# Routing's choice in two parts, norms of window units ahead of maxima, and weight splits behind the second block's norms

## The reference, cut to what matters

```python
D_MODEL, SEQ, DEPTH = 1024, 512, 2
M_GROUPS, M_PER_GROUP, M_TOPK, M_HIDDEN = 4, 8, 2, 512      # 32 experts

def first_block(x, ...):
    alpha, h = (2 * DEPTH) ** 0.25, x
    for i in range(DEPTH):
        y = swa_sink_gqa(h, ...) if i == 0 else mla(h, ...)   # window attention; latent attention
        h = layer_norm(alpha * h + y, ln_g[i, 0], ln_b[i, 0])
        y = hier_moe(h, ...)
        h = layer_norm(alpha * h + y, ln_g[i, 1], ln_b[i, 1])
    return h

def hier_moe(x, w_group, w_expert, w_gate, w_up, w_down):
    p_group = jax.nn.softmax((xt @ w_group).astype(jnp.float32), axis=-1)
    g_w, g_idx = lax.top_k(p_group, 1)
    e_logits = (xt @ w_expert).astype(jnp.float32).reshape(n_tok, M_GROUPS, M_PER_GROUP)
    e_logits = e_logits[jnp.arange(n_tok), g_idx[:, 0]]
    e_w, e_idx = lax.top_k(jax.nn.softmax(e_logits, axis=-1), M_TOPK)
    weight = g_w * e_w / jnp.sum(e_w, -1, keepdims=True)
    expert = (g_idx * M_PER_GROUP + e_idx).reshape(-1)
    ...  # tokens sorted by expert, silu(x w_gate) * (x w_up) @ w_down per expert, summed per token

def second_block(x, ...):
    for l in range(DEPTH):
        h = rms_norm_2(x, norm_mix_pre[l])
        ...  # h @ w_in, four mixers side by side, mix = concatenation @ w_out
        x = x + rms_norm_2(mix, norm_mix_post[l])
        f = conv_ffn(rms_norm_2(x, norm_ffn_pre[l]), ffn_up[l], ffn_conv_w[l], ffn_down[l])
        x = x + rms_norm_2(f, norm_ffn_post[l])
    return x

def reference(...):
    return second_block(first_block(x, ...), ...)
```

## Time and profile before

| | |
|---|---|
| median of 3 runs | 2722.62 us (2719.04, 2725.57, 2722.62) |
| the profiled execution | 2721.77 us |
| its span, first to last instruction | 2719.9 us |
| mean granted clock of TensorE | 0.976 |
| PE busy | 2500.8 us, 92% |
| PE weight loads busy | 1849.2 us, 68% |
| DVE busy | 1074.3 us, 39% |
| ACT busy | 753.2 us, 28% |
| POOL busy | 181.6 us, 7% |
| DMA traffic | 576.56 MB, mean 212 GB/s |

### The profile page before, as it was taken

One profiled execution on the slowest core, in us unless ns is written; L12 is line 12 of the kernel. 1 busy time (PEld: TensorE's weight loads), 2 busy tenths in 40 slices (PEclk: granted clock), 3 DMA queues, 4 the chain that ended last, 5 costly groups with the idle time before them and its releaser, 6 DMA issues. The chain is left out here.

```text
span 2719.9 us, 36818 instructions
## 1 busy us (share of the span) xinstructions
PE 2500.8 (92%) x14582; PEld 1849.2 (68%) x14582; DVE 1074.3 (39%) x1596; ACT 753.2 (28%) x1217; POOL 181.6 (7%) x302
## 2 busy tenths in 40 slices
PE   8997998887898979998877999999999999999998
PEld 7675665544476666654444777888887877888887
DVE  4753100100345641110001666655543566555542
ACT  3530000000245410000001353443432444433421
POOL 0001111111000001111111010000000010000000
PEclk9998999999999989999999999999999999999999
DMA  6239999999722189999998412223233212223231
GB/s 170 83 136 379 405 404 407 411 408 407 264 93 78 40 332 406 402 406 408 407 411 338 159 62 83 82 94 99 93 124 108 84 49 96 84 94 99 93 124 54
DMA packets 174825, 576.56 MB, mean 212 GB/s; under 512 B 20496, under 2 KB 104016, under 8 KB 125042
## 3 DMA queue, kind: packets, MB, share of 16 engines
q1 hardware_dynamic: 164146, 558.07, 54.1%
q0 software_dynamic: 10560, 16.81, 1.9%
HBM read 569.56 MB, written 23.07 MB: 218 GB/s over the span
## 5 line engine op out<-in xcount | busy, mean ns | idle before, releaser
L1310 PE MATMUL ps<-first_weights,moe_xsT 128*64 128x256 f32 x2688 | 311.7, 381 | 50.0 <-DMA first_weights<-in_moe_w_up 30.7
L232 PE MATMUL ps<-l_h_hi,l_w_hi 128*128 128x512 f32 x896 | 353.4, 394 | 0.0
L234 PE MATMUL ps<-l_h_hi,l_w_lo 128*128 128x512 f32 x896 | 349.2, 390 | 0.0
L233 PE MATMUL ps<-l_h_lo,l_w_hi 128*128 128x512 f32 x896 | 349.1, 390 | 0.0
L1389 DVE TENSOR_TENSOR moe_hid<-moe_silu,ps 128x256 f32<-128x256 f32 x64 | 27.0, 421 | 781.4 <-PE ps L1310 781.4
L1310 PEld LDWEIGHTS ps<-first_weights,moe_xsT 128*64 128x64 f32 x2688 | 224.1, 137 | 147.5 <-issue 97.8
L2837 DVE TENSOR_TENSOR l_w_lo<-l_raw,l_w_hi 128x2048 fp32r<-128x2048 f32 x76 | 174.1, 2293 | 270.1 <-ACT l_w_hi L2598 270.1
L1362 ACT ACTIVATE moe_ys<-ps 128x512 f32<-128x512 f32 x64 | 38.2, 597 | 684.3 <-PE ps L1328 684.3
L1328 PE MATMUL ps<-first_weights,moe_hidT 128*64 128x512 f32 x672 | 172.1, 658 | 38.7 <-DVE moe_hidT L1391 38.7
L2598 ACT ACTIVATE l_w_hi<-l_raw 128x2048 fp32r<-128x2048 f32 x76 | 145.5, 1918 | 179.5 <-PE ps L234 168.4
L232 PEld LDWEIGHTS ps<-l_h_hi,l_w_hi 128*128 128x128 f32 x896 | 168.3, 188 | 37.3 <-issue 2.9
(11 more groups left out here) (578 smaller groups left out, 4344.2 us busy)
## 6 DMA issues: line engine op xcount, KB each, us to landing
first_weights<-in_moe_w_up SPq DMA_DIRECT2D x84, 1024.0 KB, 28.6
first_weights<-in_moe_w_down SPq DMA_DIRECT2D x84, 1024.0 KB, 28.7
first_weights<-in_moe_w_gate SPq DMA_DIRECT2D x84, 1024.0 KB, 27.9
first_ring<-in_moe_w_up SPq DMA_DIRECT2D x44, 1024.0 KB, 28.7
first_ring<-in_moe_w_down SPq DMA_DIRECT2D x44, 1024.0 KB, 28.5
l_raw<-in_ffn_up SPq DMA_DIRECT2D x44, 1024.0 KB, 5.1
first_ring<-in_moe_w_gate SPq DMA_DIRECT2D x40, 1024.0 KB, 28.2
l_raw<-in_w_in SPq DMA_DIRECT2D x22, 1024.0 KB, 5.2
```

The lines of the kernel that those rows point to most:

```text
L232: pe.matmul(out, stationary[0], moving[0], start=first, stop=False)
L233: pe.matmul(out, stationary[0], moving[1], start=False, stop=False)
L234: return pe.matmul(out, stationary[1], moving[0], start=False, stop=last)
L1310: ins = pe.matmul(k.ps[64 * h:64 * h + 64, 2 + m, 0:256], xsT[:, j, :], piece[:, j % 4, 256 * h:256 * h + 256], start=j == 0, stop=j == ND ...
```

## The change

It moves work on ACT and DVE, and on PE and SP at the very end of the program. The instructions that it touches are listed here by part.

- **Window layer, DVE.** `norms(6)` stands ahead of `maxes(7)`. `am.norm` of tile 0 is cut in two: `am.centre` behind `norms(13)`, `am.finish` behind `norms(14)`.
- **Latent layer, DVE.** `low(10)` and `low(11)` move from the ends of iterations 2 and 3 to iterations 3 and 4, between `maxes(u + 1)` and `norms(u + 1)`.
- **Routing, both layers.** `choose` is called twice, for tiles 0 to 2 and for tile 3. Tile 3's logits go to PSUM bank 6. ACT takes both halves of tile 3's turned rows, DVE none. What `oht` and `oh` took in one instruction each now takes one per tile.
- **Second block.** ACT loads the table set with Sqrt ahead of the wait for the first tile, at four places. At the end of the first layer the splits of w_in pieces 0 and 1 follow `finish(0)` and `finish(1)` instead of preceding them.
- **The end.** The last tile's last down pieces are done half by half (512 columns). DVE multiplies by the gain while ACT squares, and then does scale and addition in one instruction for each half, where it did a scale and an addition of 1024 columns. The last tile's squares are summed by halves. The output leaves in eight DMAs of 256 KB instead of four of 512 KB.

```diff
@@ Router.logits, choose
-            ins = pe.matmul(k.ps[:, 0, t * P:t * P + NL], self.hT[:, j, t * P:(t + 1) * P], self.w[:, j, :], start=j == 0, stop=j == ND - 1)
+            bank, at = (0, t * P) if t + 1 < NT else (6, 0)
+            ins = pe.matmul(k.ps[:, bank, at:at + NL], self.hT[:, j, t * P:(t + 1) * P], self.w[:, j, :], start=j == 0, stop=j == ND - 1)
...
-        dve.wait_ge(x.made, NT)
-        link(dve.tensor_copy(x.gl[:, :, 0:GROUPS], lg[:, :, 0:GROUPS]))
-        link(each(dve.max(x.gm[:, t, :], x.gl[:, t, :]) for t in range(NT)))
+        dve.wait_ge(x.made, ts.stop)
+        link(dve.tensor_copy(x.gl[:, ts, 0:GROUPS], lg[:, :, 0:GROUPS]))
+        link(each(dve.max(x.gm[:, t, :], x.gl[:, t, :]) for t in tiles))
...
-        link(dve.tensor_tensor(x.oht[:, :, :], k.const(C_I32, 32).unsqueeze(1).to_broadcast([P, 8, EXPERTS]),
-                               x.ef[:, :, :].rearrange("p c t -> p (c t)").unsqueeze(2).to_broadcast([P, 8, EXPERTS]), ALU.is_equal))
-        dve.tensor_copy(x.oh[:, :, :], x.oht[:, :, :]).then_inc(x.chosen, 1)
+        link(each(dve.tensor_tensor(oht[:, :, t, :], k.const(C_I32, 32).unsqueeze(1).to_broadcast([P, TOPK, EXPERTS]),
+                                    x.ef[:, :, t].unsqueeze(2).to_broadcast([P, TOPK, EXPERTS]), ALU.is_equal) for t in tiles))
+        each(dve.tensor_copy(oh[:, :, t, :], oht[:, :, t, :]) for t in tiles).then_inc(x.chosen, 1)
@@ both layers, ACT and DVE
-            take_turned(k, copy, act, rt, 3, 0)
+            for half in range(2):
+                take_turned(k, copy, act, rt, 3, half)
...
-            take_turned(k, dve.tensor_copy, dve, rt, 3, 1)
-            rt.choose(k, dve, link, r)
+            dve.wait_ge(am.normed, NT)
+            rt.clear_choice(dve, link)
+            rt.choose(k, dve, link, (0, 1, 2))
+            rt.choose(k, dve, link, (3,))
+            rt.number(k, dve, link)
             rt.lay(k, dve, link, r)
@@ window layer, DVE
+            norms(6)
             maxes(7)
-            norms(6)
...
+                if u == 13:
+                    am.centre(k, dve, 0, k.resid[:, 0, :])
+                if u == 14:
+                    am.finish(k, dve, 0)
...
-                if u == 12:
-                    am.norm(k, dve, 0)
@@ latent layer, DVE
                     maxes(u + 1)
+                if u in (3, 4):
+                    low(7 + u)
...
-                if u in (2, 3):
-                    low(8 + u)
@@ second block, ACT (DVE the same with low)
-            def finish_all(g, made):
+            def finish_all(g, made, after):
+                act.preload_act_table_set("sqrt_and_others")
                 finish(g, 0, made)
+                after(0)
                 finish(g, 1, made)
                 split_high(g, 0)
+                after(1)
                 finish(g, 2, made)
...
-                    high(l + 1, 0)
-                    high(l + 1, 1)
-                    finish_all(ending[l], x.down_made)
+                    finish_all(ending[l], x.down_made, lambda n: high(l + 1, n))
@@ second block, the end: DVE, and SP
+            def finish_last(g):
...
+                        dve.tensor_tensor(xn[:, :], tile_banks(t), end_gains[0][:, :], ALU.mult).then_inc(by_gain, 2)
...
+                    inverse_root(g, 0, t)
+                    dve.wait_ge(by_gain, 2 * t + 2)
+                    for half in range(2):
+                        part = slice(half * 512, half * 512 + 512)
+                        dve.scalar_tensor_tensor(k.resid[:, t, part], xn[:, part], rs[:, r, 0, t:t + 1], k.resid[:, t, part], ALU.mult, ALU.add).then_inc(g.added, 1)
...
-                sp.wait_ge(ending[-1].added, t + 1)
-                sp.dma_start(k.out[0, t * P:(t + 1) * P, :], k.resid[:, t, :]).then_inc(stored, 16)
+                for half in range(2):
+                    part = slice(half * 512, half * 512 + 512)
+                    sp.wait_ge(ending[-1].added, 2 * t + half + 1)
+                    sp.dma_start(k.out[0, t * P:(t + 1) * P, part], k.resid[:, t, part]).then_inc(stored, 16)
```

116 lines of the change are left out of this document (78 added, 38 removed).

## The result

The changed kernel takes 2706.34 us (median of 4 runs, 2703.84 to 2707.08) against 2721.34 for the kernel before (median of 4, 2719.04 to 2725.57). The ratio is 0.9939, with a 95% interval from 0.9925 to 0.9952: faster by 13 to 20 us. That lies inside the forecast range of 2696 to 2711. 19.25 us were forecast, against the medians 15.0 were found. The profiled execution takes 2706.22 us, with a span of 2704.4.

A forecast was written before the change was run, and what follows sets the result against it. The weight stream was taken to bound the two expert stages and PE the rest, with DVE and ACT costing only where PE waits. Terms summed to 19.25 us off 2721.77, giving 2702.5 us, range 2696 to 2711.

The forecast's parts named there:

- End of the first layer: Second block: earlier table load and later w_in splits remove PE's 5.80 us wait and the slow clock behind it; 7.5 us.
- w_out: Second block: loading the table ahead of the wait removes PE's 0.60 us wait at two places; 1.2 us.
- The end: Program end: last tile squared, scaled and sent by halves, so it finishes sooner after PE is done; 1.6 us.
- Norm of tile 0: Window layer: cutting this norm in two lets norms(13) come earlier and removes PE's wait; 2.05 us.
- `norms(6)` first: Window layer: norms(6) ahead of maxes(7) removes PE's 2.11 us wait, partly offset by later maxima; 1.6 us.
- Latent layer: Moving low(10) and low(11) behind the maxima shortens PE's 4.08 us wait; 2.4 us.
- Routing, window: Window layer: choosing for three tiles first ends `choose` earlier and passes to the end; 0.8 us.
- Routing, latent: Latent layer: three tiles' choice hides wholly before late logits, and the load stream restarts earlier; 2.1 us.
- Rival 1: Gains ahead of the expert stages are lost in them, leaving 10.3 us and a time of 2711.5; chance 0.14.
- Rival 3: PE's clock stays up behind the shorter waits, above all in the latent layer; 1.7 to 3 us more, 2700; chance 0.10.
- Rival 4: Expert stages: earlier loads meet other transfers and cut the rate by 3%; slower, 2731; chance 0.02.
- Rival 5: Routing: three tiles' part doesn't overlap PE's last logits, so both Routing terms fall away; 2706.4; chance 0.04.

The follow-up runs named there:

- e7: Changed kernel plus seven extra DVE copies (2.1 us in all) ahead of tile 3's choice in the latent layer; 2706.74 us, ratio 0.9955.
- e1: Kernel before with the Routing part (split choice) alone; 2722.00 us against 2720.96, ratio 1.0006.
- e5: Changed kernel with Routing as before, one choice for all four tiles; 2704.25 us, ratio 0.9943 to the kernel before.
- e9: Changed kernel with maxes(7) ahead of norms(6) as before, the cut norm of tile 0 kept; 2704.66 us, ratio 0.9937.
- e12: Changed kernel run once more, unaltered, to see its own spread; 2704.67 us, ratio 0.9937.
- e11: Kernel before with only the second block's parts, including the last tile by halves; 2709.42 us against 2721.16, ratio 0.9952.
- e4: Changed kernel with the store of the last tile's rows behind three of six loads instead of all six, both layers; 2703.53 us, ratio 0.9933.
- e8: Changed kernel with the last 1 MB load of the latent layer's burst moved behind the block's end; 2706.66 us, ratio 0.995.

## Why the prediction was right, and where not

The range held and the direction was right; the sum was high by some 3 to 4 us. It held because the second block, over half of the sum, was priced well. Of the 4.5 us that were put on `norms(6)` and the two Routings, next to nothing arrived, and only a range of 15 us had room for that. By its steps:

- **What bounds the kernel**: right. Every gain found came from a wait of PE that the timeline names and the clock behind it, or from the end.
- **End of the first layer, 7.5**: 8.1. The mechanism is as described, down to the room of under 1 us for the first turn. The splits delay no turn.
- **w_out, 1.2**: right, the waits are gone. **The end, 1.6**: 1.9.
- **Table load**: it now runs at 2055.36, in ACT's idle time. The changed kernel's root follows its square as it did behind the load before. The price of 1.28 us held, and the drain that the Trainium skill adds in "ScalarE: Activation LUTs", section "What ACT_TABLE_LOAD costs", shows in no row here.
- **Norm of tile 0, 2.05**: right (about 96.95 to 94.75 and 94.90).
- **`norms(6)` first, 1.6**: the step that failed in the window layer. "`maxes(7)` then starts about when the scores are there ... and not moved up by the whole 2.1": at full clock they start 1.7 us later than before, and unit 7's turn comes at 11.62 instead of 10.91. That is a loss of 0.7, more where the clock falls behind it, and 0.1 to 0.2 of gain only where the clock is low ahead of it, as it was in the execution that the forecast read. And "All that precedes passes in the window case" didn't hold: in six of seven kernels the clock fell at the layer's last logits.
- **Latent layer, 2.4**: right in the mean (2.6); at like clock it is 2.0 to 4.4, where 1.2 to 4.1 was the bound. Which of these an execution gets isn't set by the wait's length.
- **Routing, window, 0.8**: 0.66 at the rank matmuls; 0.5 of it arrives at full clock, 1.4 at the lower. The rank matmuls' wait is 4.47 at full clock (4.3 were forecast) and 3.08 in the changed kernel, where slow logits fill the rest.
- **Routing, latent, 2.1**: the step that failed most. "In the latent layer the logits come only at 982.83, after 2.67 us of idleness" was true of one execution, at the lower clock; in the others the choice gains 0.35, and the wait is 4.77 where 3.0 was forecast. With the logits done after 3.4 us, the three tiles' part isn't hidden wholly. And "so the stream starts again earlier by what Routing is earlier" is wrong: e7's delay of 2.2 us shifts nothing. The first expert matmul follows the gathered rows, and these land when the burst ahead has drained, not when the list is done. The forecast read the gap behind the burst and overlooked that the small transfers had to get through the burst first.
- The rule weighed there, that many small instructions pay a fixed latency each ("VectorE: DVE Perf Modes" of the Trainium skill, section on the TRN2 errata), agrees with the traces: tile 3's own part takes 2.97 us for 15 small instructions, where the whole for four tiles took 4.96. e1's total, 1.0006 (0.9997 to 1.0015), shows neither the loss that the rule alone would give nor a gain.
- **Rival 1** holds for the latent Routing, and by another mechanism than the one written: not the bound stream behind, but the burst in front. **Rival 3** was seen in the latent layer, in two of nine executions (e5, e9). Rival 4 wasn't seen: from the first expert matmul to the combining one, the latent layer's stage takes 490.0 us in the kernel before and 490.4 in the changed one. Rival 5 came out near in time, but not in mechanism: DVE's part for three tiles does run beside PE's last logits.

Put together: 11.2 from the second block, 2.6 from the latent layer, 2.0 from the window layer with its Routing and nothing from the latent Routing give 15.8. The ratio of the first comparison gives 16.6 with an interval of 13 to 20, the medians 15.0 there and 16.5 in e12. The part ahead of the second block, 4.6 of this sum, is what lies between e11 and e12, 4.8.

What stays open: why the clock falls in one execution and not in the next of the same program; whether the norms ahead of the maxima bring the slow logits at the end of the window layer; and so whether the split choice is worth its place without them. One profiled execution of each kernel stands behind every interval. The medians of e4, e5 and e9 lie 1.7 to 2.8 us under the changed kernel's first one and 0 to 1.1 under its second, inside what five runs can tell. None is shown to beat it.

## What to carry to other kernels

A wait that goes from the timeline is a gain only if the next instruction that the engine needs is ready too: follow the chain one unit further, on every engine, before counting it. Where a small transfer must pass a queue of large loads, speed up nothing ahead of it before looking up when the loads drain; a delay experiment tells in one run whether a stretch is on the path. Let the interval by which an edit is judged end behind the next thing that can take the gain back: with Routing as before, the window edits look worth 1.8 us at the last norm and 0.3 at the first expert matmul. And where the clock falls now and then, read an interval from several executions, since one of them may show a wait that the others don't have.

## What the runs showed of the hardware

The granted clock behind the same instructions and the same waits differs from execution to execution. Behind the wait of 1.70 us in the latent layer it was 0.59 over 8 us in one execution (the changed kernel) and 1.00 throughout in others (e5, e9); behind the constant wait of 2.4 us later it fell in six of fourteen kernels. The window stretch took 96.0, 96.9 or 98.7 us with the instructions of before, and 94.6 or 96.2 with both edits.

A gather of 64 rows behind a burst of queued loads of 1 MB needed 4.5 us from issue to landing in e7 and 6.8 in the changed kernel, where it was issued 2.2 us sooner: the landing stays where it is, within 0.6 us of the burst's last load. With one load fewer ahead (e8) it took 4.4. A store of 512 KB took 16.4 us behind six such loads and 7.7 behind three.

The filler between two blocks is itself subject to the clock: 4.54 us at a granted clock of 0.62 (the changed kernel), 3.44 at 0.82 (e7), and the next block's loads wait for its end.
